# Decoder block of HGRN2 and dilated attention: the output projection begun inside the last attention block, and keys of a new unit sent at another point of ACT's order

## The reference

```python
u = rms_norm(x, norm_w)
hg_q, hg_f, hg_i, hg_z, at_q, at_k, at_v, at_z = split(u @ w_in)       # eight of 512 columns
o_hg = rms_norm_per_head(hgrn2(silu(hg_q), hg_f, hg_i, lb)) * g * silu(hg_z)   # 4 heads of 128
q, k = rope(at_q), rope(at_k)                                          # 8 heads of 64
for window, dilation in ((128, 1), (512, 4), (2048, 16)):              # causal, every d-th key
    outs, lses += dilated_window_attention(q, k, v, window, dilation)
o_at = sum(softmax(lses) * outs) * silu(at_z)
h = x + concat(o_hg, o_at) @ w_out
out = rms_norm(h, final_norm_w)
```

## Time and profile before

| | us |
|---|---|
| median of 3 runs | 1422.93 (1418.78 to 1424.01) |
| profiled execution, time | 1427.43 |
| its span | 1425.6 |
| mean granted PE clock | 0.976 |
| busy: PE, DVE, ACT, POOL | 1320.9, 723.4, 466.3, 439.2 |
| from 1177.04 (scores of tile 60) to 1247.09 (end of output tile 0) | 70.1, of it PE busy 45.0, clock 0.81 |

### The profile page before, as it was taken

How to read it: one execution, slowest core, us unless ns; L and a number is a source line. 1 busy time by engine, 2 the same in 40 slices (tenths; PEclk the granted TensorE clock), 3 DMA queues, 4 the chain that set the end, 5 groups by cost and what they waited for, 6 DMA issues and landing times.

```text
span 1425.6 us, 24204 instructions
## 1 busy us (share of the span) xinstructions
PE 1320.9 (93%) x8520; PEld 1151.6 (81%) x8520; DVE 723.4 (51%) x1885; ACT 466.3 (33%) x1328; POOL 439.2 (31%) x441
## 2 busy tenths in 40 slices
PE   5999989998999999799999899989998996699997
PEld 5989989897999889699788777877786775588886
DVE  5837764783767478201555445544454453333332
ACT  5621222122122212112455345534553455322111
POOL 5733334243234212202242234323432332112100
PEclk9999999999999999999999999999999998799999
DMA  6520132022012202330454355435543456434441
GB/s 207 146 78 20 47 94 70 29 69 93 19 45 78 84 18 91 93 98 29 116 149 123 95 130 137 122 89 132 141 118 96 121 128 185 148 117 142 142 139 59
DMA packets 120688, 143.91 MB, mean 101 GB/s; under 512 B 20352, under 2 KB 86400, under 8 KB 120576
## 3 DMA queue, kind: packets, MB, share of 16 engines
q1 hardware_dynamic: 118176, 138.46, 34.2%
q10 hardware_dynamic: 2400, 3.93, 1.0%
HBM read 87.56 MB, written 29.62 MB: 82 GB/s over the span
## 4 chain that ended last, share of the span: by engine, by line
PE 43%; DMA 7%; DVE 2%; issue 2%; POOL 1%; SPq 1%; ACT 1%; ACTq 0%; POOLq 0%; DVEq 0%
PE bank L607 5%; PE bank L609 5%; PE bank L608 5%; PE bank L740 5%; PE bank L742 5%; PE bank L741 5%; PE bank L848 3%; PE bank L795 3%; PE bank L788 2%; DMA qd<-turned 2%; PE bank L840 2%; PE bank L809 1%; DMA far_v<-values 1%; PE bank L817 1%; DMA tab<-in_rope 1%
## 5 line engine op out<-in xcount | busy, mean ns | idle before, releaser
L607 PE MATMUL bank<-w_hi,u_hi 128*128 128x256 f32 x768 | 222.6, 290 | 9.2 <-POOL w_lo L1123 4.9
L608 PE MATMUL bank<-w_lo,u_hi 128*128 128x256 f32 x768 | 219.1, 285 | 0.0
L609 PE MATMUL bank<-w_hi,u_lo 128*128 128x256 f32 x768 | 219.0, 285 | 0.0
L607 PEld LDWEIGHTS bank<-w_hi,u_hi 128*128 128x128 f32 x768 | 149.2, 194 | 11.6 <-POOL w_lo L1123 5.3
L1302 DVE TENSOR_TENSOR room<-room 128x256 f32<-128x256 f32 (+6 forms) x386 | 133.9, 395 | 41.4 <-POOL room L1187 37.7
L608 PEld LDWEIGHTS bank<-w_lo,u_hi 128*128 128x128 f32 x768 | 149.3, 194 | 0.2
L609 PEld LDWEIGHTS bank<-w_hi,u_lo 128*128 128x128 f32 x768 | 149.1, 194 | 0.0
L740 PE MATMUL bank<-u_hi,w_hi 128*128 128x512 f32 x256 | 110.7, 432 | 4.0 <-issue 4.0
L1302 DVE TENSOR_TENSOR t<-bank,tab 128x512 f32<-128x512 f32 x64 | 42.5, 685 | 134.8 <-PE bank L742 55.7
L607 PE MATMUL bank<-u_hi,w_hi 128*128 128x512 f32 x256 | 101.9, 398 | 7.5 <-issue 4.8
L607 PE MATMUL bank<-wo_hi,mT_hi 128*128 128x512 f32 x256 | 102.1, 399 | 4.8 <-DVE mT_lo L1302 4.8
(11 more groups left out here) (166 smaller groups left out, 2965.2 us busy)
## 6 DMA issues: line engine op xcount, KB each, us to landing
qd<-turned SPq DMA_DIRECT2D x64, 256.0 KB, 4.8
stage<-in_w_groups SPq DMA_DIRECT2D x44, 256.0 KB, 3.7
room<-in_x SPq DMA_DIRECT2D x16, 512.0 KB, 4.4
values_gates<-vg_tile SPq DMA_DIRECT2D x64, 128.0 KB, 1.7
room<-values_gates SPq DMA_DIRECT2D x16, 512.0 KB, 4.5
tab<-in_rope SPq DMA_DIRECT2D x16, 512.0 KB, 6.0
wide<-mix_weights SPq DMA_DIRECT2D x32, 256.0 KB, 3.9
xr<-in_x SPq DMA_DIRECT2D x16, 512.0 KB, 4.8
```

What stands on the lines that cost most here:

```text
L607: nc.tensor.matmul(dst, lhs_hi(k), rhs_hi(k), start=(k == 0), stop=False)
L608: nc.tensor.matmul(dst, lhs_hi(k), rhs_lo(k), start=False, stop=False)
L609: last = nc.tensor.matmul(dst, lhs_lo(k), rhs_hi(k), start=False, stop=(k == KT_N - 1))
```

## The change

It has two parts.

1. In the last tile of a unit's fourth block, ACT's two key gathers stand right behind `take_near(T - 1)`, ahead of the exponentials.
2. The output projection. Its weights and the tiles of the output stage now lie in strips of u that are dead earlier: the weights over the token columns 0 to 1023 (blocks 0 and 1 of a unit), the tiles over columns 1024 to 2047. The weights are loaded in tiles 51 to 58, one load of 512 KB each, split by ACT in tiles 53 to 60 and by POOL (odd tiles) and DVE (even tiles). In tiles 60 to 63 SP loads the first mixed, attended and residual tiles. PE turns mixed tiles 0 and 1 at the end of tiles 60 and 61 (into banks 0 and 7), and does output tile 0 and the first half of output tile 1 as fillers of tiles 61 to 64 (24 groups of three matmuls). The gate of block 15 gets its own tile (`last_gate`) and is computed in tiles 60 (ACT) and 61 (DVE) in place of 62 and 63. `y_ready` and `hsum_done` count halves of a tile, and PE waits for the half whose bank it takes. The last block's mixing and combination move by one output tile.

```diff
-        wo_hi = [at(f"wo_hi{s}", U_HI + 4096 * s, [KT_N, 512], F32R) for s in range(2)]
+        u_raw = at("u_raw", U_LO, [KT_N, SEQ])
+        wo_hi = [u_hi[:, :, 512 * s:512 * s + 512] for s in range(2)]
+        wo_lo = [u_lo[:, :, 512 * s:512 * s + 512] for s in range(2)]
+        wo_raw = [u_raw[:, :, 512 * s:512 * s + 512] for s in range(2)]
+        strips = iter([U + SEQ * k + D + 512 * z for U in (U_HI, U_LO) for k in range(KT_N) for z in range(2)])
...
+        def y_bank(t, half):
+            return ((bank[0], bank[7]) if t == 0 or t % 2 else (bank[3], bank[6]))[half]
+        def turn_bank(t):
+            return (bank[0], bank[7])[t] if t < 2 else bank[1 + t % 2]
# SP
             def load_out_weights(j):
+                after(z_ready, AT_BLOCKS - 3 + j // 4)
...
-                if n == AT_BLOCKS - 1 and i < 2:
+                if AT_TILES - 13 <= T < AT_TILES - 5:
+                    load_out_weights(T - (AT_TILES - 13))
+                if T == AT_TILES - 4:
                     after(z_ready, AT_BLOCKS)
-                    for j in range(4 * i, 4 * i + 4):
-                        load_out_weights(j)
+                    after(comb_stored, 16 * (AT_BLOCKS - 3))
+                    for t in range(2):
+                        load_mixed(t)
+                        load_attended(t)
+                    load_residual(0)
+                if T == AT_TILES - 3:
+                    load_residual(1)
+                    load_mixed(2)
+                    load_attended(2)
...
                 if T == AT_TILES - 2:
                     sp.dma_start(fw[:, :], final_w).then_inc(fw_landed, 16)
-                    for t in range(MX_SLOTS):
-                        load_mixed(t)
-                        load_residual(t)
+                    load_mixed(3)
+                    load_residual(2)
+                if T == AT_TILES - 1:
+                    load_residual(3)
# PE
+            def output_matmuls(t, half, k):
+                if k == 0:
+                    pe.wait_ge(mlo_done, t + 1)
+                    if t == 0:
+                        pe.wait_ge(wo_lo_pool, 2 * half + 2)
+                        pe.wait_ge(wo_lo_dve, 2 * half + 2)
+                        if half == 1:
+                            pe.wait_ge(mlo_done, 2)
+                    elif t == 1:
+                        pe.wait_ge(hsum_done, half + 1)
+                    elif t == 2:
+                        pe.wait_ge(s_taken, 4 * AT_TILES)
+                        pe.wait_ge(o_read, AT_TILES)
+                    else:
+                        pe.wait_ge(hsum_done, 2 * (t - 2) + half + 1)
...
+            out_fill = [(t, half, k) for t, half in ((0, 0), (0, 1), (1, 0)) for k in range(KT_N)]
+            def between(T, first, many):
+                if T <= AT_TILES - 4:
+                    return itertools.chain.from_iterable(filler_matmuls(*f) for f in fillers(T, first, many))
+                at_ = 6 * (T - (AT_TILES - 3)) + first - 2
+                return itertools.chain.from_iterable(output_matmuls(*f) for f in out_fill[max(at_, 0):at_ + many])
...
                 if T >= 1:
                     weigh(T - 1)
+                if T in (AT_TILES - 4, AT_TILES - 3):
+                    mixed_transposes(T - (AT_TILES - 4))
+            run(between(AT_TILES, 0, 2))
             turn_near_far0(AT_TILES - 1)
+            run(between(AT_TILES, 2, 2))
             turn_far1(AT_TILES - 1)
+            run(between(AT_TILES, 4, 4))
             weigh(AT_TILES - 1)
# ACT
+            def mixed_hi(t):
+                act.wait_ge(at_landed[t % AT_SLOTS], 16 * (t // AT_SLOTS + 1))
+                if t >= 2:
+                    act.wait_ge(y_ready, 2 * (t - 1))
+                nc.scalar.copy(mT_hi[t % 2][:, 4:8, :], at_in[t % AT_SLOTS][:, :, :])
+                act.wait_ge(mT_mm, t + 1)
+                nc.scalar.copy(mT_hi[t % 2][:, 0:4, :]..., turn_bank(t)[:, :]).then_inc(mhi_done, 1)
                 if T >= 1:
                     take_near(T - 1)
+                if i == 3 and g == 3 and n + 1 < AT_BLOCKS:
+                    act.wait_ge(s_ready, 3 * T + 3)
+                    act.wait_ge(qk_lo, n + 2)
+                    gather_keys(nc.scalar, n + 1, (0,))
                 if T < AT_TILES:
                     exps(T, 0)
...
-                if i == 3 and g == 3 and n + 1 < AT_BLOCKS:      # behind take_output
-                    act.wait_ge(s_ready, 3 * T + 3)
-                    act.wait_ge(qk_lo, n + 2)
-                    gather_keys(nc.scalar, n + 1, (0,))
...
+                if AT_TILES - 11 <= T < AT_TILES - 3:
+                    out_weights_hi(T - (AT_TILES - 11))
+                if T in (AT_TILES - 4, AT_TILES - 3):
+                    mixed_hi(T - (AT_TILES - 4))
# DVE
+                if T == AT_TILES - 3:
+                    mixed_lo(0)
...                                                              # lows(T, 0), take_far0(T - 1), lows(T, 1)
+                if T == AT_TILES - 2:
+                    mixed_lo(1)
+                    residual(0, 0)
+                if AT_TILES - 11 <= T < AT_TILES - 3 and T % 2 == 0:
+                    out_weights_lo(T - (AT_TILES - 11))
             take_far0(AT_TILES - 1)
+            residual(0, 1)
```

More of the change, by code:

```diff
@@ new lines, in _, with run @@
+            out_fill = [(t, half, k) for t, half in ((0, 0), (0, 1), (1, 0)) for k in range(KT_N)]
[4 more added lines that the diff above has]
+                return itertools.chain.from_iterable(output_matmuls(*f) for f in out_fill[max(at_, 0):at_ + many])
+            def run(matmuls):
+                for _ in matmuls:
+                    pass
@@ new lines, in mixed_transposes @@
+            def mixed_transposes(t):
+                pe.wait_ge(mx_landed[t % MX_SLOTS], 16 * (t // MX_SLOTS + 1))
+                if t == 0:
+                    pe.wait_ge(z_done, AT_BLOCKS - 1)
+                elif t == 1:
+                    pe.wait_ge(z_done, AT_BLOCKS)
+                elif t < 4:
+                    pe.wait_ge(s_taken, 4 * AT_TILES)
+                else:
+                    pe.wait_ge(mlo_done, t - 1)
+                for k in range(4):
+                    last = nc.tensor.transpose(turn_bank(t)[:, k * P:(k + 1) * P], mx[t % MX_SLOTS][:, k * P:(k + 1) * P], ident[:, :])
+                last.then_inc(mT_mm, 1)
@@ L859, in _ @@
             for T in range(AT_TILES):
-                scores(T, itertools.chain.from_iterable(filler_matmuls(*f) for f in fillers(T, 0, 2)))
+                scores(T, between(T, 0, 2))
                 if T % CH == 1 and T > CH:
@@ L864, in _ @@
                     turn_near_far0(T - 1)
-                for f in fillers(T, 2, 2):
-                    filler(*f)
+                run(between(T, 2, 2))
                 if T >= 1:
                     turn_far1(T - 1)
-                for f in fillers(T, 4, 2):
-                    filler(*f)
+                run(between(T, 4, 2))
                 if T >= 1:
                     weigh(T - 1)
+                if T in (AT_TILES - 4, AT_TILES - 3):
+                    mixed_transposes(T - (AT_TILES - 4))
@@ L886, in _ @@
[L886 to L891 removed]
+            for t in range(1, TILES):
                 if t + 1 < TILES:
                     mixed_transposes(t + 1)
[L894 removed]
+                if t == 3:
                     turn_weights(AT_BLOCKS - 1)
[L896 to L906 removed]
+                for half in range(1 if t == 1 else 0, 2):
+                    for k in range(KT_N):
+                        run(output_matmuls(t, half, k))
@@ L1073, in _ @@
                     queries_keys_hi(n + 1)
-                if i == 2:
+                if i == (0 if n == AT_BLOCKS - 1 else 2) and T < AT_TILES:
                     act.wait_ge(z_ready, n + 1)
-                    if n >= 1:
+                    if 1 <= n < AT_BLOCKS - 1:
                         act.wait_ge(comb_done, n)
-                    nc.scalar.activation(gate[:, :], bank[filler_bank("Z", n)][:, :], ACT.Tanh, scale=0.5).then_inc(th_done, 1)
+                    nc.scalar.activation(gate_of(n), bank[filler_bank("Z", n)][:, :], ACT.Tanh, scale=0.5).then_inc(th_done, 1)
                 for z in {0: (T - 1,), 1: (), 2: (T - 2, T - 1), 3: (T - 1,)}[i]:
@@ L1265, in _ @@
                     combine(n - 1)
-                for j in {AT_TILES - 2: (0,), AT_TILES - 1: (2,), AT_TILES: (4, 6)}.get(T, ()):
-                    out_weights_lo(j)
+                if AT_TILES - 11 <= T < AT_TILES - 3 and T % 2:
+                    out_weights_lo(T - (AT_TILES - 11))
             nc.gpsimd.memset(o_half[:, :], -0.5).then_inc(pool_step, 1)
@@ L1631, in _ @@
+            for t in range(2, TILES + 2):
                 if t < TILES:
-                    dve.wait_ge(mhi_done, t + 1)
-                    tt(mT_lo[t % 2][:, 4:8, :], at_in[t % AT_SLOTS][:, :, :], mT_hi[t % 2][:, 4:8, :].bitcast(F32), ALU.subtract)
-                    tt(mT_lo[t % 2][:, 0:4, :].rearrange("p a b -> p (a b)"), bank[1 + t % 2][:, :],
```

(17 more changed lines are left out.)

128 lines of the change are left out of this document (53 added, 75 removed).

## The result

The changed kernel takes 1387.8 us at the median of four runs (1384.8 to 1390.8), against 1422.9 before: ratio 0.975 (95%: 0.973 to 0.977). The forecast was 1378 in 1366 to 1398: direction and range held, the gain came out at 35 us and not 45. The profiled execution took 1390.8 (span 1389.0), where the sum had its like at 1382.1.

What follows compares the result with a forecast made beforehand. PE, busy 93%, bounds the kernel, losing time and clock at unit changes and in the last block. Terms -18.7 - 29.0 + 3 - 0.6 = -45.3 give 1382.1 profiled, 1378 from the 1422.9 median; range 1366 to 1398.

Steps and rivals of the forecast that it cites:

- rival 1: Last block still waits for distant values behind output-stage loads; gain 18 instead of 29, time 1389; chance 0.15.
- Part one, keys: Unit changes after tiles 15, 31, 47: keys sent sooner gain 18.7 us, bounds 0 to 22.6.
- Rival 2: Unit changes: keys land no sooner, held up by SP's traffic; gain near 0, time 1397; chance 0.10.
- The last block: Scores of tile 60 to end of output tile 1: 81.4 us becomes 52.4, gain 29.0, bounds 18 to 33.7.
- the first lows: Tile 61: first output matmuls wait 0.7 us for both halves of the split mixed tile.
- Rivals 1 and 5: rival 1, and: output matmuls of tiles 61 to 64 only wait for operands; part two gains 5, 1402, chance 0.06.
- The output stage: Residuals and bank releases by halves after the loop: no PE wait before, so 0 us change.
- rival 4: Output stage: finer hand-over makes DVE the bound; at 4 us more per tile 1434, slower; chance 0.03.
- recorded signs of being wrong: 4 us waits at clock 0.5, query waits above 3 at tiles 52, 56 or 60, or output tile above 11.5.
- The tail: Very end: the sum behind the last matmul, 1.29 us, becomes one half; gain 0.6.
- Weight loads and splits in tiles 51 to 60: Loads make queries late at block changes 52, 56, 60: 3 us lost, bounds 0 to 6; splits cost nothing.
- So they are hidden: Splits in tiles 53 to 60 cost nothing: ACT busy 3.8 of 7.0 us, DVE 2.5, POOL 0.

Runs made afterwards that it cites:

- e1: The changed kernel itself, unedited, measured a second time: median 1385.8 us, ratio 0.973.
- e2: The kernel before with only ACT's key gathers moved earlier at tiles 15, 31 and 47: median 1402.5 us, ratio 0.984.
- e4: The changed kernel with whole weight loads but splits on ACT, POOL and DVE cut to 32 of 512 columns: 1386.5 us, ratio 0.975.
- e12: The changed kernel with mixed tile 1 split earlier in tile 62, last mixing weights turned in output tile 4, DVE's weight splits one tile later: 1380.5 us, 0.966.
- e9: The changed kernel itself, unedited, measured a third time: median 1389.6 us, ratio 0.973.
- e8: The changed kernel with both weight loads and splits cut to 32 columns: median 1379.8 us, ratio 0.970.

## Why the prediction was right, and where its size was off

Direction and range held, and both mechanisms came as described. The median of 1387.8 lies outside the forecast's own narrower range (1371 to 1386) and next to rival 1's 1389. The median can't tell the two apart; the traces can, since rival 1's waits in the last block are not there. By the books below one term is 8.7 us off; two smaller errors, of 2.7 and -2.8, cancel by luck. One trace could also have flattered the sum: e1's profiled execution (1384.0) is 43.4 us below the kernel before's, nearly the 45.3 forecast, while the three medians gain 35.1 to 38.6.

- **Part one, keys: right.** Predicted -18.7; the three changes went from 48.24 to 29.27 us, -19.0 (-19.6 in e2's trace). The residual wait was put at 1.3 each; it is 3.1 in three. At the third change of the changed kernel the keys leave at 1054.75, behind the copy of the turned near scores, and PE waits little:

```profile
1054.69 0.59 ACT L1084 COPY pT<-bank 128x512 f32<-128x512 f32 x1 [1.89 <-PE bank L880]
1054.75 1.81 ACTq L333 DMA_DIRECT2D ks<-turned  x2
...
1061.25 0.66 PE L859 MATMUL bank<-ks,qd 128*128 128x128 f32 x4 [0.99 <-DMA ks<-turned]
```

  Rival 2 is refuted: the keys do land sooner, and e2's queries are not later. The Trainium skill ("DMA: Bandwidth & Descriptors", "Issuing engines are not separate DMA queues") has transfers of all engines share the same 16 DMA engines. This trace agrees: while the keys were under way the share was 0.89, and ACT's two gathers took 5.2 us to land at the median, where they took 3.9 in the kernel before, at a share of 0.46 while they were waited for.

```profile
1054.75:1061.25 6.50, 5.51 (x44) 4.42 (x42) 2.69 (x9) 3.88 (x11) 0.15 (x1) 1.00 0.89 224
```

  So sharing takes back some 1.3 us of landing time, if it is that. The gain is of another kind: seen from the near weighing (1058.25 here, 1073.48 before) the gathers leave 5.6 us sooner.
- **The last block: right to 2 us.** Predicted 52.4 us from the scores of tile 60 to the end of output tile 1, measured 54.28. Its waits came where they were named: for mixed tile 0 0.2 us in this trace and 1.2 in e1 (2.0 was put), for the first lows 0.48 (0.7), for the second 2.20 (2.0), none for distant values in tiles 61 to 63 (0). The first lows, by the timeline of PE:

```profile
1178.12 0.50 PE L788 MATMUL bank<-u_hi,mT_hi 128*128 128x512 f32 x1 [0.48 <-DVE mT_lo L1361]
```

  From the end of tile 60's first stage (1182.90 before, 1172.78 now) to the end of output tile 1 PE takes 48.4 us, 45.1 of them busy, where it took 75.5 (64.19 + 11.35) with 51.3 busy. Rivals 1 and 5 are refuted: distant values hold nothing up behind tile 60, and the output matmuls wait 2.7 us in all. That stretch isn't free of the low clock: its windows have 0.83 and 0.96, where the sum had the high clock. PE is busy 50.2 us in them (5.07 + 45.12), some 3 more than the sum had, and stands still somewhat less than it had: the 2 us missed are clock, not waits.
- **The output stage: 0 predicted, 1.3 lost once.** Tile 2 takes 11.37 us, so the hand-over by halves costs nothing and rival 4 is refuted. Tile 3 takes 13.15. Of the 1.8 us above the others 0.5 is the turn of the mixing weights itself, which before lay in output tile 2 (11.87 from transposes to transposes); the wait of 1.22 ahead of it was overlooked. So one of the recorded signs of being wrong (an output tile above 11.5) did appear, for a reason that no rival had named. The change moved PE's turn from t == 2 to 3 and DVE's mixing from 1 to 3, so the one met the other. I had read the edit and priced its instructions, not the distance between the two.
- **The tail: right.** The sum behind the last matmul is 0.69 us instead of 1.29:

```profile
1381.79 0.69 DVE L1361 TENSOR_TENSOR hh<-bank,xr 128x512 f32<-128x512 f32 x1 [4.75 <-PE bank L790]
```

- **Weight loads and splits in tiles 51 to 60: mis-sized.** Predicted +3 in bounds of 0 to 6; 11.7, 3.6 and 16.3 in three traces, mean 10.5. This is the term that failed. The part of it that was priced, late queries at changes of block, is there: waits for them of 1.8, 0.6 and 4.8 us in this stretch, for 1.0 before. Two sentences of it were wrong. "So they are hidden", of the splits: the row it rested on had DVE busy 2.5 of 7.0 us, which says nothing of what stands behind a split in DVE's order; e4 and e12 bring tile 53 from about 9 back to 7.4, the one by cutting the splits, the other by moving DVE's alone. And the loads were priced as late queries alone, at the bandwidth. In the trace they also delay what is small and needed soon: distant values at tile 58, and at tile 55 the statistics, stored ahead of a load and behind another (landing 4.0 us at the median in this trace, 4.9 in e9, but 2.5 in e1; 2.8 before). There three delays in a row make a stretch at half clock, by the timeline and a window:

```profile
1128.11 0.47 SPq L586 DMA_DIRECT2D far_stats<-st_far  x1
...
1132.14 0.36 SPq L512 DMA_DIRECT2D st_farn<-far_stats  x1
```

```profile
1139.26 1.22 DVE L1361 TENSOR_TENSOR u_lo<-u_raw,u_hi 128x1024 fp32r<-128x1024 f32 x1
1139.41 0.39 PE L927 MATMUL bank<-ident,w 128*16 128x128 f32 x2 [1.53 <-DVE w L1630]
...
1141.72 0.27 DVE L1638 COPY wide<-bank 16x128 f32<-16x128 f32 x1
1142.14 0.87 PE L888 MATMUL bank<-ident,p_far 128*128 128x128 f32 x3 [1.75 <-DVE wide L1638]
```

```profile
1142.00:1145.00 3.00, 2.86 (x9) 2.40 (x10) 1.71 (x7) 1.09 (x4) 1.78 (x1) 0.50 0.01 3
```

  The statistics are read back 4.0 us after they were stored, the weights made of them come late (1.53), DVE's split stands (with two steps of rope) ahead of the copy that the next turn needs (1.75), and after these 3.3 us of waiting PE runs at 1.2 GHz. The same place in e1 is the comparison: there the statistics are read back after 2.55 us, PE doesn't wait for the weights, waits the same 1.74 for the copy, and the clock stays at 1.00. A third error is in the sum's form: the term had no price for the clock, and 4.3 of this trace's 11.7 us are matmuls at less than the high clock. Which of the loads delays which small transfer was read from the order on SP, not tested one by one.

**The books.** From the forecast for the profiled execution (1382.1) to what it took (1390.8) there are 8.7 us: weights +8.7 (11.7 for 3), all from weighing 59 on +2.7 (26.9 gained for 29.6), the rest of tiles 3 to 48 +0.4, part one -0.3, and -2.8 in the part ahead of tile 3, which the change doesn't touch.

**What stays open:** why the transfers land later in one execution than in another. What follows from that is shown: the waits for queries, mixing weights and distant values make 1.3, 2.1, 6.7 and 10.1 us in the kernel before, e1, the changed kernel and e9, and PE's busy time in the stretch 78.8, 78.3, 83.1 and 85.0 at mean clocks of 1.00, 1.00, 0.95 and 0.92. The granted clock of whole executions agrees: of e9's six the slowest (1397.8 us, the one traced) has a mean granted clock of 0.986 and the fastest (1382.0) 0.995.

## What to carry to other kernels

An engine that is busy a third of the time still isn't cover for a new instruction: look at what the instruction waits for, and at what stands behind it in order that a busier engine waits for. Price a large load by the small transfers just behind it, not by its bytes alone. When two engines hand something over by iteration numbers and an edit moves both, check the distance that is left between them. And take two or three traces where waits for DMAs decide: three traces of one program gave 86.6 to 99.3 us for the same stretch.

## What the runs showed of the chip that was not expected

Short waits were enough for the low clock. At the scores of tile 24 of the changed kernel PE waited 1.83 us for queries, by its timeline and two windows (columns as above):

```profile
854.22 0.51 PE L859 MATMUL bank<-ks,qd 128*128 128x256 f32 x2 [1.83 <-DMA qd<-turned]
```

```profile
853.00:856.00 3.00, 1.78 (x7) 1.62 (x8) 0.64 (x2) 0.40 (x1) 2.46 (x2) 0.82 0.31 89
856.00:859.00 3.00, 3.00 (x14) 2.52 (x13) 0.65 (x2) 0.03 (x1) 0.00 (x0) 0.61 0.34 58
```

From the weighing of tile 22 to that of 23 it took 11.27 us, where e1 without a wait took 7.96: 1.8 for the wait and 1.5 for matmuls at the low clock. Behind the wait of 0.99 at the third change of unit the clock stayed at 1.00.

Nor does the same wait always have the same price. In tile 62 PE waits 2.20 us for mT_lo in eight of the traces, in the same place of the same order. The 3 us behind it, in the changed kernel and in e1:

```profile
1191.97:1194.97 3.00, 3.00 (x14) 2.12 (x15) 0.45 (x1) 0.00 (x0) 0.00 (x0) 0.64 0.05 18
1186.74:1189.74 3.00, 3.00 (x27) 2.46 (x28) 0.46 (x1) 0.00 (x0) 0.00 (x0) 1.00 0.02 5
```

Six traces have a clock of 0.50 to 0.75 there, e1 and e8 1.00. From the transposes of mixed tile 1 to those of mixed tile 2 the six take 31.6 to 31.7 us and the two 30.1: the low clock costs 1.5 to 1.6 us, behind one and the same wait. So a wait of some 2 us can cost nearly its own length again, and does not always; every wait of 4 us or more between 700 and 1250 us was followed by 3 us at 0.50 to 0.52. What decides between the two for the short ones stays open.

And DVE's path to the mixing weights holds 2 us that no wait of PE names. By the timeline of the changed kernel, in tile 55 and behind the loop's last rope:

```profile
1135.99 2.54 POOL L1275 TENSOR_TENSOR r<-t,t 64x512 f32<-64x512 f32 x1 [5.08 <-DVE t L1361]
1136.46 2.08 DVE L1361 TENSOR_TENSOR den<-ea,st_near 128x8 f32<-128x8 f32 x1
...
1173.77 0.17 DVE L1361 TENSOR_TENSOR den<-ea,st_near 128x8 f32<-128x8 f32 x1 [0.82 <-ACT eb L1105]
```

This addition of 128x8 elements takes 2.1 us in each of the 14 blocks in which it starts while POOL runs that product of rope, and ends within 0.03 us of it; in the last two blocks, with no rope, it takes 0.17. The traces of the kernel before, e1 and e8 have the same. Where an instruction is small and its time is long, look at what runs beside it.
